# Two weight units of a mixture-of-experts stage, loaded by sixteen transfers of eight partitions each

## The reference

```
layer 0: x = x + dilated_attention(rmsnorm(x));   x = x + swiglu(rmsnorm(x))            # d_ff 2816
layer 1: x = x + multiscale_pooling(rmsnorm(x));  x = x + moe_swiglu(rmsnorm(x))        # 8 experts, top 2
out = rmsnorm(x)

def swiglu(h, w_gate, w_up, w_down):
    return (silu(h @ w_gate) * (h @ w_up)) @ w_down
```

## Time and profile before

| | us |
|---|---|
| median of three runs | 1356.46 (1355.63 to 1356.54) |
| the profiled execution | 1358.75 |
| its span, first to last instruction | 1357.0 |
| TensorE busy (matmul) | 1314.3, 97% of the span |
| VectorE busy | 427.5, 32% |
| ScalarE busy | 305.1, 22% |
| moved by DMA | 447.45 MB, 330 GB/s over the span |

### The profile page before, as it was taken

One profiled execution on the slowest core, in us unless ns is written; L12 is line 12 of the kernel. 1 busy time (PEld: TensorE's weight loads), 2 busy tenths in 40 slices (PEclk: granted clock), 3 DMA queues, 4 the chain that ended last, 5 costly groups with the idle time before them and its releaser, 6 DMA issues.

```text
span 1357.0 us, 31023 instructions
## 1 busy us (share of the span) xinstructions
PE 1314.3 (97%) x13973; PEld 941.6 (69%) x13973; DVE 427.5 (32%) x719; ACT 305.1 (22%) x467; POOL 80.2 (6%) x76
## 2 busy tenths in 40 slices
PE   7999999999999999999999999999989999999985
PEld 7999999878888886665556666665546666665543
DVE  6987878965444560000000000000000000000002
ACT  5455455554444460000000000000000000000002
POOL 1511111010000000000000000000000000000000
PEclk9999999999999999999999999999999999999998
DMA  9644454357665578999999999999999999999993
GB/s 355 250 166 151 147 187 184 128 180 280 248 245 218 182 284 358 372 386 403 419 412 419 417 421 406 420 418 406 419 421 412 419 418 405 421 418 418 408 420 152
DMA packets 68425, 447.45 MB, mean 330 GB/s; under 512 B 7920, under 2 KB 10608, under 8 KB 16192
## 3 DMA queue, kind: packets, MB, share of 16 engines
q1 hardware_dynamic: 63456, 436.57, 80.1%
q0 software_dynamic: 4400, 8.30, 2.3%
q10 hardware_dynamic: 432, 0.54, 0.1%
HBM read 438.70 MB, written 6.68 MB: 328 GB/s over the span
## 4 chain that ended last, share of the span: by engine, by line
PE 89%; DMA 5%; SPq 4%; ACT 1%; DVE 1%; issue 1%; ACTq 0%; DVEq 0%
PE bank L1783 37%; PE bank L1802 14%; PE bank L444 10%; PE bank L446 10%; PE bank L445 10%; SPq L465 3%; DMA raw_late<-in_expert_units 2%; DMA w_raw<-in_expert_units 2%; PE bank L1730 2%; PE bank L1546 1%; PE bank L1528 1%; PE bank L1561 1%; PE bank L1762 1%; DMA qkT<-in_xT 1%; PE bank L1536 0%
## 5 line engine op out<-in xcount | busy, mean ns | idle before, releaser
L400 DVE TENSOR_TENSOR w_lo<-raw,w_hi 128x2048 fp32r<-128x2048 f32 x70 | 160.5, 2293 | 60.6 <-ACT w_hi L395 60.4
L395 ACT ACTIVATE w_hi<-raw 128x2048 fp32r<-128x2048 f32 x71 | 135.9, 1914 | 90.1 <-PE bank L446 84.1
L444 PE MATMUL bank<-w_hi,a_hi 128*128 128x256 f32 (+1 forms) x400 | 136.5, 341 | 1.0 <-DVE a_lo L1154 0.5
L446 PE MATMUL bank<-w_hi,a_lo 128*128 128x256 f32 (+1 forms) x400 | 133.9, 335 | 0.0
L445 PE MATMUL bank<-w_lo,a_hi 128*128 128x256 f32 (+1 forms) x400 | 133.9, 335 | 0.0
L1280 DVE TENSOR_TENSOR h<-sg,bank 128x384 f32<-128x384 f32 (+1 forms) x56 | 28.2, 504 | 301.8 <-PE bank L1802 163.1
L1286 DVE COPY hT_x<-bank 128x128 f32<-128x128 f32 x35 | 10.1, 290 | 352.3 <-ACT hT_x L842 352.3
L444 PE MATMUL bank<-a_hi,w_hi 128*128 128x256 f32 x384 | 112.4, 293 | 8.6 <-DVE w_lo L982 8.6
L446 PE MATMUL bank<-a_hi,w_lo 128*128 128x256 f32 x384 | 110.2, 287 | 0.0
L445 PE MATMUL bank<-a_lo,w_hi 128*128 128x256 f32 x384 | 110.2, 287 | 0.0
L842 ACT ACTIVATE hT_x<-bank 128x256 f32<-128x256 f32 x35 | 13.4, 383 | 420.1 <-PE bank L1730 420.1
(11 more groups left out here) (302 smaller groups left out, 1861.0 us busy)
## 6 DMA issues: line engine op xcount, KB each, us to landing
w_raw<-in_expert_units SPq DMA_DIRECT2D x86, 1024.0 KB, 28.1
raw<-in_units SPq DMA_DIRECT2D x71, 1024.0 KB, 4.9
raw<-in_expert_units SPq DMA_DIRECT2D x60, 1024.0 KB, 27.6
raw_more<-in_expert_units SPq DMA_DIRECT2D x45, 1024.0 KB, 27.4
raw_late<-in_expert_units SPq DMA_DIRECT2D x45, 1024.0 KB, 27.6
extra<-in_expert_units SPq DMA_DIRECT2D x30, 1024.0 KB, 26.9
a_raw<-in_expert_units SPq DMA_DIRECT2D x28, 1024.0 KB, 26.5
aside_raw<-in_expert_units SPq DMA_DIRECT2D x15, 1024.0 KB, 27.5
```

The lines of the kernel that those rows point to most:

```text
L395: nc.scalar.activation(w_hi[:, u % SPLIT, :], where, ACT.Copy).then_inc(hi_ready, 1)
L400: nc.vector.tensor_tensor(w_lo[:, u % SPLIT, :], home(u)[0], w_hi[:, u % SPLIT, :].bitcast(F32), ALU.subtract).then_inc(lo_ready, 1)
L444: nc.tensor.matmul(bank, hi, w[0], start=start, stop=False)
L446: return nc.tensor.matmul(bank, lo, w[0], start=False, stop=stop)
```

## The change

Units 150 and 250 are loaded in another way. Unit 150 is unit 24 at position 3, and unit 250 is unit 40 at position 5 (both wide). Each is loaded by sixteen transfers. The transfer `at` (0 to 15) takes the partitions at, at + 16, ..., at + 112, eight in number, 8 KB each, 64 KB in all. Each transfer adds 16 to the place's semaphore, so the unit adds 256; `landings` now counts these, and TensorE waits for the sum. The waits of SP, the places, the order and the bytes are as before, and all other units are loaded by one transfer each.

```diff
+BY_EIGHT = (150, 250)
-def uses_before(n):
-    return SLOT_OF[:n].count(SLOT_OF[n])
+def landings(slot, n):
+    return sum(P // 8 if _m in BY_EIGHT else 1 for _m in range(n) if SLOT_OF[_m] == slot)
...
                 n = i * UE + j
-                slot, landings = SLOT_OF[n], uses_before(n) + 1
+                slot = SLOT_OF[n]
+                lands = landings(slot, n + 1)
             else:
                 slot = j % AGAIN
-                landings = SLOT_OF.count(slot) + UE // AGAIN * (i - E) + j // AGAIN + 1
-            return ring[slot], ring_landed[slot], landings * 16
+                lands = landings(slot, MAIN) + UE // AGAIN * (i - E) + j // AGAIN + 1
+            return ring[slot], ring_landed[slot], lands * 16
...
+            def load_by_eight(src, home):
+                where, landed, _value = home
+                for at in range(P // 8):
+                    sp.dma_start(where[at::P // 8].rearrange("p (k n) -> p k n", k=src.shape[1]), src[at::P // 8]).then_inc(landed, 16)
...
-                load(expert_source(j, e), expert_home(i, j))
+                if n in BY_EIGHT:
+                    load_by_eight(expert_source(j, e), expert_home(i, j))
+                else:
+                    load(expert_source(j, e), expert_home(i, j))
```

## The result

The change made the kernel slower. The median went from 1356.46 us to 1380.56 us (five runs each), a ratio of 1.0186 with a 95% interval of 1.0172 to 1.0200. The profiled execution has a span of 1380.1 us, 23.1 us more than before. The forecast was 1351.5 us with a range of 1350.3 to 1361.8 us, so the sign was wrong and the time lies outside the range. One execution of the kernel before, in the first group of the experiments, took 7547 us and is left out.

What follows compares the result with a forecast made beforehand. DMA was taken to bound the last expert, TensorE the wide experts before, with eight engines lagging at the end. Sparing these 5.0 us gave a span of 1357.0 - 5.0 = 1352.0 us, median 1351.5 us, range 1350.3 to 1361.8 us.

Steps and rivals of the forecast that it cites:

- What bounds the kernel: Last expert: DMA limits it, at 2.50 us a unit against TensorE's 1.73; TensorE limits the wide experts before.
- A transfer of eight partitions ... at most eight engines carry it: Units 150 and 250: each narrow transfer is eight packets of 8 KB, so at most eight engines carry it.
- the same eight: Units 150 and 250: all 32 narrow transfers fall on the same eight engines, the lowest-numbered by the skill.
- These are the eight that lead: End of stage: leading engines carry the narrow transfers, lagging ones are spared 5.0 us; last landing 1335.75, not 1340.75 us.
- I take 0.312 us, since all rows at full share have it: Packet time in a narrow transfer, as now; forecast whole up to 0.335 us, gain gone at 0.49 us.
- Rival 2: Narrow transfers: several engines write close together, packets take twice as long, leading eight end at 1345 us; 1360.7 us, 11%.
- their combination with the lagging engines: Narrow transfers on the lagging eight and double packet times together, 1371 us; left outside the range.
- rival 1: Narrow transfers fall on the lagging eight engines; the lag grows by 5.0 us, last landing 1345.75 us; 1361.5 us, 18%.
- The completions: Each leading engine posts 15 more completions a unit; between nothing and 1.5 us in all, taken as nothing.
- A later landing while TensorE is the bound: Both units are wanted before 981 us and between 1028 and 1279 us; landing some us later costs nothing.
- SP waits for no release: After 800 us SP waits for no release, so the queue of loads doesn't hang on TensorE.
- SP's issues: Sixteen issues at 0.48 us take 7.7 us a unit, SP 5.5 us late, covered by the queue; counted as nothing.

Runs made afterwards that it cites:

- lower half's kernel: Against the kernel before: units 150, 200, 250, 300 load only partitions 0 to 63, in eight transfers of eight partitions four apart; 1355.11 us, ratio 0.9993.
- upper half's kernel: Against the kernel before: units 150, 200, 250, 300 load only partitions 64 to 127, in eight transfers of eight partitions four apart; 1378.23 us, ratio 1.0158.

## Why the prediction was wrong, step by step

- **What bounds the kernel** was right: DMA bounds the last expert, and the last landing moved by 23.0 us with the span's 23.1. TensorE's lead in the middle hid nothing of the loss.
- **"A transfer of eight partitions ... at most eight engines carry it", "the same eight"** was right as far as the runs can tell: 224 packets more, and the lower and the upper half differ as they do if it is always the same eight.
- **"These are the eight that lead"** failed in part. Two of them lag. With their doubled load these two set the end (the step of 0.12), so the balance got worse by 3.6 us where it was to get better by 5.0.
- **"I take 0.312 us, since all rows at full share have it"** failed, and is most of the error. Every such row is of whole loads, in which each engine writes its own partitions; they could not speak for others. Measured were about 0.6 us in the stretches concerned (0.616 us at 1.03 and 219 GB/s). The rule of the Trainium skill ("SBUF — State Buffer", on the port swizzle) that was set against the rows was the better guide: by it the eight engines reach four of sixteen ports, and the packets did crowd.
- **Rival 2** had the mechanism, and the wrong size: 4.25 us against 24. It charged the doubled time to the narrow packets of the leading eight, and took for granted that the other engines go on at their rate. They slowed as well: 244 and 255 GB/s in place of 420, for 20 and 30 us, which is 20.2 us of DMA time. The top of the range rested on that step. The range left their combination with the lagging engines (1371 us) outside, and both came, if rival 1 only for two of the eight.
- **The completions** at nothing: no run prices them alone, but 32 transfers in the lower half's kernel cost no time. **A later landing while TensorE is the bound**, at nothing, rested on TensorE staying the bound. It didn't: it waited 1.80 us for a landing in `a_raw` at 1141 us, and the chain is at landings and issues for most of 943 to 1167 us. That was named as a sign of a wrong forecast. The waits themselves added nothing, since the last landing and the span moved by the same 23 us. **SP waits for no release** was right (0.4 us). **SP's issues** took 14.7 and 18.5 us for a unit, twice what was worked out, and were covered as foreseen but for some 0.7 us. In the lower half's kernel the eight issues of a unit took 11.7 us with the rate at 418 to 422 GB/s.
- Some readings were loose, and nothing hung on them. In the slices of 830 to 860 us the lowest rate is 382 GB/s, not 404. The nines of the DMA share begin with the seventeenth slice, not the sixteenth, and the rates there are 372 to 421 GB/s, not 403 to 423. Two issues in 5.17 us are 2.6 us each, not 2.2.

What stays open: why engines that write only their own partitions slow down when others cross. The packets' times show that they do (all 103 that start between 856 and 860 us in the upper half's kernel took 0.54 us or more), but no run separates a shared way into SBUF from one in front of it. Why adjacent partitions lose 5 us less than sixteen apart in traffic, though their packets take longer alone, is not explained either. That the lag comes from the instruction queue fits in size (13.6 us against 12.8) but was not tried.

## What to carry to other kernels

Load whole tiles of 128 partitions, or parts that spread over all of SBUF in the same pattern (32 partitions four apart were free). By the reading above, a part that lets an engine write partitions which belong to another in the other loads in flight slows all 16 engines while it lasts, here from 420 to between 205 and 300 GB/s; 1 MB loaded so cost 6 to 12 us more, where 2.5 us is its whole price. When DMA is the bound, price a new transfer's shape by what it does to the loads beside it, and don't take its packet time from rows of another shape.

## What was not expected of the hardware

- Eight transfers of 16 partitions, or two of 64, each carried by all 16 engines, cost 11.7 and 15.8 us for two units: an ordinary split of a load in halves is not free.
- Narrow transfers of partitions 0 to 63, four apart, cost no time (1355.11 against 1355.39 us, with 2 MB less to load), and those of 64 to 127 cost 23 us.
- While unit 7's narrow transfers of adjacent partitions were under way in the dense part, all engines stood at a share of 1.04 and moved 131 GB/s, 1.04 us for a packet, over three times the usual.
- SP needed 0.9 to 1.5 us for an issue of 64 KB in full traffic (16 in 14.66 us, eight in 11.71 us) and 0.36 to 0.67 us in the dense part (16 in 5.81 to 10.69 us), and the DMA engines are not even at the end of a long run of equal loads: eight of them ended 12.8 us ahead of the others, in the mean.
